# DeltaNet chunk inversion in four batches of five same-direction matrices, half of the columns, Y as the transpose of X

## The chip, the cores and the metric

The kernel runs on one core of a Trainium2 chip. The metric is the device time of one launch in microseconds (us). The kernel before was run three times.

## What is computed

One layer of a hybrid backbone: a gated DeltaNet in both directions over 1024 latent and 256 context tokens, windowed attention, a merge of the two, and a convolutional FFN. The change sits in the DeltaNet, which works head by head (8 heads of width 128). The part of the reference that matters is the triangular solve within a chunk:

```python
diff = gc[..., :, None] - gc[..., None, :]
decay = jnp.where(incl, jnp.exp(jnp.where(incl, diff, 0.0)), 0.0)
kk = jnp.einsum('nbhid,nbhjd->nbhij', kc, kc)
a_mat = jnp.where(strict, bc[..., :, None] * kk * decay, 0.0)
sol = lax.linalg.triangular_solve(a_mat, rhs, left_side=True, lower=True, unit_diagonal=True)
```

The kernel takes chunks of 128 tokens (10 of them) and, for each chunk and direction, inverts the unit triangular 128x128 matrix B itself, lower or upper by the direction. That is 20 inverses for each head.

## The kernel before

**Stages of a head.** `pe_prepare`, `dve_body`, `act_body` and `pool_body` hold the code of a head on the four engines. A head has four stretches: preparation (transposes, decays, the 20 matrices B in `b_full`, and a half precision copy `b_half`), the inversion (`pe_inverse`), one refinement of the inverse in full precision (the second half of `pe_inverse`), and the chain over the chunks (`pe_chain`), among whose steps the projections of the next head are laid (`pe_group`). A head's inversion waits for its preparation, and its chain for its refinement; nothing of another head lies beside the inversion on TensorE.

**The inversion.** X approaches the inverse of B by doubling the size of the diagonal blocks that are already inverted, in seven levels (block size 1, 2, ... 64); Y is kept as the transpose of X, since TensorE wants one operand transposed. A level makes P = B X, keeps the blocks of P that this level adds (a mask on VectorE, `p_masked`), and adds their product to X and Y. `BT` = 5 batches hold four 128x128 matrices each: two chunks, both directions. Level 0 needs only the mask (`x_half`), and Y of level 0 is a masked copy of B that GpSimd makes (`first_y`, L1743).

- TensorE, `p(n)` (L1274): 4 matmuls of 128 columns. `xy(n)`: X passed through an identity into PSUM (L1285, 512 columns), 4 matmuls of 128 columns on top (L1287), and the same for Y (L1289, L1291).
- VectorE, L1629: mask of 512 columns from PSUM to half precision, one for each batch and level.
- ScalarE, L1468 and L1469: X and Y back from PSUM, 512 columns each; in the last level as full precision, for the refinement.
- GpSimd, L1763: in the last level a half precision copy of Y.

Each engine runs its own list in order. `Count` objects are semaphores that only grow; `.wait` names the count to be reached. On TensorE `p` runs one batch ahead of `xy`, so that a mask has the time of one `xy` to be made:

```python
for n in range(BT + N + 1):
    if n < BT + N:
        p(n)
    if n >= BT + 1:
        xy(n - BT - 1)
```

**The refinement.** For each batch: residual product in full precision (L1306), its rounding on VectorE (L1637), a product with Y (L1317), the sum on VectorE (L1645).

**GpSimd.** `pool_body` copies the head's columns (L1723), makes two `g_masked` (L1732), puts ones on the diagonal of B as each batch comes (`affine_select`, L1749), the first Y, then splits the next head's weight tile for K (L177, L184). The tile for V is split only after the refinement, as `y_full` lies in its slot.

## Time and profile before

| | us |
|---|---|
| median of 3 runs | 3272.65 (3272.5 to 3274.65) |
| span of the profiled execution | 3268.6 |
| TensorE busy (matmul) | 2928.3, 90% |
| VectorE busy | 1503.2, 46% |
| ScalarE busy | 904.8, 28% |
| GpSimd busy | 700.1, 21% |

The span runs from the first to the last instruction of one profiled execution; the median of the timed runs is 4.05 us longer, which is what lies around the span. Matmuls are pipelined, and their records last longer than they hold the array, so the distance from start to start counts rather than their length. LDWEIGHTS, the load of the stationary operand, is a record of its own (PEld). PEclk is the granted clock as a share of 2.4 GHz.

### The profile page before, as it was taken

To read this page: it belongs to the slowest core of one execution; us is meant where nothing else is said; L and a number is where in the kernel's file an instruction comes from. 1 tells how busy PE (TensorE), PEld (TensorE's weight loads), DVE (VectorE), ACT (ScalarE), POOL (GpSimd) and SP (SyncE) were. 2 spreads that over 40 slices of the span, in tenths; PEclk is the share of its full clock that TensorE was granted. 3 is DMA by queue.
4 is the path that set the end of the run, shared out by engine and by line. 5 is a ranking of instruction groups with operands and counts; after the bars stand their busy time and mean duration, and the time that the engine had idled before them with its cause. 6 is when DMAs were issued, how large, how long until landed. Compare 5 with 4: busy or idle time off the path is not lost. (4 is left out here: it accounts for less than half of the span.)

```text
span 3268.6 us, 46436 instructions
## 1 busy us (share of the span) xinstructions
PE 2928.3 (90%) x17000; PEld 2430.4 (74%) x17000; DVE 1503.2 (46%) x2475; ACT 904.8 (28%) x1546; POOL 700.1 (21%) x545
## 2 busy tenths in 40 slices
PE   8599999799899899989899898869695999997999
PEld 7477788687678787878787777758574888886877
DVE  1474444300546565656565656631213555555242
ACT  1421333200251525252534343310113121222010
POOL 0241000132221213121212122023221232322221
PEclk7799899799889898999999899879897999998999
DMA  4110221221100001000000000032222111111433
GB/s 190 54 34 5 84 97 65 90 78 47 43 8 7 27 8 34 17 18 21 14 21 14 21 14 7 1 123 103 103 86 82 51 46 50 47 49 55 125 117 102
DMA packets 41784, 176.28 MB, mean 54 GB/s; under 512 B 4624, under 2 KB 4880, under 8 KB 39696
## 3 DMA queue, kind: packets, MB, share of 16 engines
q1 hardware_dynamic: 39312, 169.78, 15.4%
q10 hardware_dynamic: 2304, 4.20, 0.3%
q8 instruction: 114, 1.87, 0.2%
q14 instruction: 54, 0.44, 0.0%
HBM read 148.79 MB, written 25.17 MB: 53 GB/s over the span
## 5 line engine op out<-in xcount | busy, mean ns | idle before, releaser
L194 PE MATMUL ps_up<-h_hi,up_w_hi 128*128 128x512 f32 x704 | 274.6, 390 | 37.5 <-POOL up_w_lo L184 37.5
L195 PE MATMUL ps_up<-h_lo,up_w_hi 128*128 128x512 f32 x704 | 274.4, 390 | 0.0
L196 PE MATMUL ps_up<-h_hi,up_w_lo 128*128 128x512 f32 x704 | 274.4, 390 | 0.0
L1189 PE MATMUL dn_bank<-h_hi,dn_w_hi 128*128 128x512 f32 (+1 forms) x640 | 244.7, 382 | 12.8 <-POOL dn_w_lo L184 12.8
L1189 PE MATMUL dn_bank<-h_lo,dn_w_hi 128*128 128x512 f32 (+1 forms) x640 | 244.5, 382 | 0.0
L1189 PE MATMUL dn_bank<-h_hi,dn_w_lo 128*128 128x512 f32 (+1 forms) x640 | 244.4, 382 | 0.0
L1629 DVE TENSOR_TENSOR p_masked<-dn_bank,constants 128x512 f16<-128x512 f32 x240 | 165.9, 691 | 116.5 <-PE dn_bank L1274 115.5
L2017 DVE TENSOR_SCALAR ffn_u<-ffn_pad,vectors 128x1024 f32<-128x1024 f32 x44 | 103.9, 2360 | 232.2 <-ACT ffn_pad L1997 232.2
L194 PEld LDWEIGHTS ps_up<-h_hi,up_w_hi 128*128 128x128 f32 x704 | 132.6, 188 | 65.7 <-issue 38.3
L2086 PE MATMUL ps_down<-act_hi,down_w_hi 128*128 128x512 f32 x352 | 139.2, 395 | 24.4 <-DVE act_lo L2125 24.4
L195 PEld LDWEIGHTS ps_up<-h_lo,up_w_hi 128*128 128x128 f32 x704 | 132.6, 188 | 27.5
L196 PEld LDWEIGHTS ps_up<-h_hi,up_w_lo 128*128 128x128 f32 x704 | 132.5, 188 | 27.6
L1513 DVE SCALAR_TENSOR_TENSOR conv_out<-conv_in,head_taps,conv_out 128x1284 f32<-128x1284 f32 (+1 forms) x96 | 152.8, 1592 | 0.4
L1407 ACT ACTIVATE conv_in<-dn_bank 128x512 f32<-128x512 f32 (+1 forms) x64 | 34.9, 545 | 426.5 <-PE dn_bank L1189 420.2
L1189 PEld LDWEIGHTS dn_bank<-h_hi,dn_w_hi 128*128 128x128 f32 x640 | 122.1, 191 | 30.1 <-POOL dn_w_lo L184 13.2
L2087 PE MATMUL ps_down<-act_lo,down_w_hi 128*128 128x512 f32 x352 | 138.7, 394 | 0.0
L2088 PE MATMUL ps_down<-act_hi,down_w_lo 128*128 128x512 f32 x352 | 138.4, 393 | 0.0
L1468 ACT ACTIVATE x_half<-dn_bank 128x512 f16<-128x512 f32 x200 | 119.4, 597 | 59.9 <-PE dn_bank L1291 48.4
L1189 PEld LDWEIGHTS dn_bank<-h_hi,dn_w_lo 128*128 128x128 f32 x640 | 122.0, 191 | 17.0
L1189 PEld LDWEIGHTS dn_bank<-h_lo,dn_w_hi 128*128 128x128 f32 x640 | 122.1, 191 | 16.9
L184 DVE TENSOR_TENSOR down_w_lo<-down_w_raw,down_w_hi 128x1408 fp32r<-128x1408 f32 x32 | 52.0, 1626 | 161.2 <-POOL down_w_hi L177 161.2
L177 POOL CAST up_w_hi<-up_w_raw 128x1024 fp32r<-128x1024 f32 x44 | 45.7, 1039 | 371.4 <-PE ps_up L196 311.2
(317 smaller groups left out, 7122.1 us busy)
## 6 DMA issues: line engine op xcount, KB each, us to landing
up_w_raw<-in_w_up SPq DMA_DIRECT2D x44, 512.0 KB, 3.5
down_w_raw<-in_w_down SPq DMA_DIRECT2D x32, 704.0 KB, 4.2
late_w_ada<-in_w_ada SPq DMA_DIRECT2D x8, 2048.0 KB, 9.6
dn_w_raw<-in_w_dn SPq DMA_DIRECT2D x32, 512.0 KB, 3.8
w_ada<-in_w_ada SPq DMA_DIRECT2D x4, 2048.0 KB, 13.6
at_w_raw<-in_w_mg_at SPq DMA_DIRECT2D x16, 512.0 KB, 4.2
dnm_w_raw<-in_w_mg_dn SPq DMA_DIRECT2D x16, 512.0 KB, 5.2
x_in<-in_xT SPq DMA_DIRECT2D x8, 640.0 KB, 11.8
```

What stands on the lines that cost most here:

```text
L184: eng.tensor_tensor(self.lo[j][:, :, :], self.raw[j][:, :, :], self.hi[j][:, :, :].bitcast(F32), ALU.subtract).then_inc(self.split, 1)
L194: pe.matmul(out, self.hi[j][:, k, :], xh, start=(k == 0), stop=False)
L195: pe.matmul(out, self.hi[j][:, k, :], xl, start=False, stop=False)
L196: mm = pe.matmul(out, self.lo[j][:, k, :], xh, start=False, stop=(k == self.kt - 1))
L1189: mm = pe.matmul(bank[4 + s % 3][:, 0:n], wt[:, k, :], x[:, k, t0:t0 + n], start=(k == 0 and v == 0), stop=(k == KT - 1 and v == 2))
L1468: act.activation(flat(x_f if last else x_h, n % BT), bank[2 + n % 2][:, :], ACT.Copy)
L1513: ins = dve.scalar_tensor_tensor(out=dst, in0=src[:, j:j + n], scalar=taps[:, tile_at(tile), j:j + 1], in1=dst, op0=ALU.mult, op1=ALU.add)
L1629: dve.tensor_tensor(pm[:, (n - BT) % 2, :, :].rearrange("p (c d) n -> p c (d n)", c=2), p, mask, ALU.mult).then_inc(pmd.sem, 1)
L2017: ins = dve.tensor_scalar(u[:, s, :], src, tap(0), vec[:, bass.ds(m + s * FT + V_CONVB, 1)], ALU.mult, ALU.add)
L2086: pe.matmul(ps[j][:, :], w.hi[part][:, k, :], hi, start=(kk == 0), stop=False)
L2087: pe.matmul(ps[j][:, :], w.hi[part][:, k, :], lo, start=False, stop=False)
L2088: mm = pe.matmul(ps[j][:, :], w.lo[part][:, k, :], hi, start=False, stop=(kk == FT - 1))
```

## The change

A batch is now five matrices of one direction (`GC` = 5 chunks, `GB` = 4 batches). For a lower triangular X a level changes only columns in the even blocks, for an upper one only in the odd blocks; P, the mask, the product and the copy back take these 64 of 128 columns (`half`, `halves`, `packed`). Y is no longer updated by its own products: `y(n)` turns X by 5 matmuls with columns of an identity and copies the other half of the columns. X and Y start as identities that GpSimd writes (`units`). The copies of Y go by turns to ScalarE and VectorE. The last level leaves X in half precision; GpSimd widens the refinement's batches 0, 2 and 4 (`xfp`), ScalarE 1 and 3 (`xfa`), and the refinement adds to the half precision Y. GpSimd splits the next V tile before the end of the inversion. The constants lose nine 128x128 matrices.

```diff
         unit = 1.0 * (r == c) if level == 0 else 0.0
-        mats += [unit - m, unit - m.T]
-    mats += [mats[C_LEVEL + 1], mats[C_LEVEL]]
+        even = (np.arange(P) // s) % 2 == 0
+        mats.append(np.concatenate([(unit - m)[:, even], (unit - m.T)[:, ~even]], 1))
     mats = np.stack([np.broadcast_to(m, (P, P)) for m in mats], 1).astype(np.float32)
...
         size = NCH * 2 * P * 2
-        x_h, y_h = place("x_half", [P, NCH, 2, P], 0, F16), place("y_half", [P, NCH, 2, P], size, F16)
-        pm = place("p_masked", [P, 2, 4, P], 2 * size, F16)
-        e_h = place("residual_half", [P, 2, 4, P], 2 * size + 2048, F16)
-        b_h = place("b_half", [P, NCH, 2, P], cv_bytes, F16)
-        x_f = place("x_full", [P, NCH, 2, P], cv_bytes + size, F32)
-        y_full = [nc.alloc_sbuf_tensor_at(f"y_full{j}", [P, 2, 4 * P], F32, offset=ring + slot * tile_bytes)
-                  for j, slot in enumerate((Weights.HI + 1, Weights.LO + 1))]
-        y_f = [y_full[0][:, 0, :], y_full[0][:, 1, :], y_full[1][:, 0, :], y_full[1][:, 1, :],
-               o_norm[:, 0:4, :].rearrange("p m n -> p (m n)")]
-        assert 2 * size + 4096 <= cv_bytes and size * 3 <= pad_bytes + 2 * line
+        x_f = place("x_full", [P, NCH, 2, P], 0, F32)
+        pm = place("p_masked", [P, 2, GC, P // 2], 2 * size, F16)
+        e_h = place("residual_half", [P, 2, 4, P], 2 * size + 2560, F16)
+        x_h, y_h = place("x_half", [P, NCH, 2, P], cv_bytes, F16), place("y_half", [P, NCH, 2, P], cv_bytes + size, F16)
+        b_h = place("b_half", [P, NCH, 2, P], cv_bytes + 2 * size, F16)
+        assert 2 * size + 2560 + 2048 <= cv_bytes and size * 3 <= pad_bytes + 2 * line
         bank = [core.ps(f"dn_bank{b}", [P, HALF], ctx=st) for b in range(8)]
...
             return t[:, 2 * bt:2 * bt + 2, :, :]
+        def half(t, c, di, s, odd):
+            return t[:, c, di, :].rearrange("p (b two s) -> p b two s", two=2, s=s)[:, :, odd, :]
+        def halves(t, q, s, odd):
+            g, di = q // 2, q % 2
+            return t[:, g * GC:(g + 1) * GC, di, :].rearrange("p c (b two s) -> p c b two s", two=2, s=s)[:, :, :, odd, :]
+        def packed(b, s):
+            return bank[b][:, 0:GC * P // 2].rearrange("p (c b s) -> p c b s", c=GC, s=s)
...
+            def y_made(n):
+                if n % 2:
+                    ydv.wait(pe, h * YHALF + n // 2 + 1)
+                else:
+                    yac.wait(pe, h * YHALF + n // 2 + 1)
+            def x_made(n):
+                if n < GB:
+                    x1d.wait(pe, h * GB + n + 1)
+                else:
+                    xev.wait(pe, h * MSTEPS + n - GB + 1)
...
+                lv, q = divmod(n, GB)
+                g, di = q // 2, q % 2
...
+                    bhd.wait(pe, h * 5 + (5 if g else 3))
+                else:
+                    x_made(n - GB)
+                if 2 <= n < GB + 2:
+                    x1d.wait(pe, h * GB + n - 1)
+                elif n >= GB + 2:
+                    pmd.wait(pe, h * MSTEPS + n - GB - 1)
+                for i in range(GC):
+                    c = g * GC + i
+                    x = half(x_h, c, di, 1 << lv, di) if lv else core.id_h[:, di:P:2].unsqueeze(2)
+                    mm = pe.matmul(packed(n % 2, 1 << lv)[:, i], b_h[:, c, di, :], x, start=True, stop=True)
...
+            def x(n):
+                lv, q = divmod(n, GB)
+                g, di = q // 2, q % 2
+                pmd.wait(pe, h * MSTEPS + n - GB + 1)
+                y_made(n - GB)
+                if n >= GB + 2:
+                    xev.wait(pe, h * MSTEPS + n - GB - 1)
+                o = packed(2 + n % 2, 1 << lv)
+                pe.matmul(o, core.id_h[:, :], halves(x_h, q, 1 << lv, di), start=True, stop=False)
+                for i in range(GC):
+                    mm = pe.matmul(bank[2 + n % 2][:, i * P // 2:(i + 1) * P // 2], y_h[:, g * GC + i, di, :], pm[:, n % 2, i, :],
+                                   start=False, stop=(i == GC - 1))
+                mm.then_inc(xp.sem, 1)
+            def y(n):
+                lv, q = divmod(n, GB)
+                g, di = q // 2, q % 2
+                x_made(n)
+                if n >= 2:
+                    y_made(n - 2)
+                else:
+                    unit.wait(pe, h + 1)
+                turn = core.id_h[:, :].rearrange("p (b two s) -> p b two s", two=2, s=1 << lv)[:, :, 1 - di, :]
+                for i in range(GC):
+                    mm = pe.matmul(packed(6 + n % 2, 1 << lv)[:, i], x_h[:, g * GC + i, di, :], turn, start=True, stop=True)
+                mm.then_inc(yp.sem, 1)
+            for n in range(STEPS + 3):
+                if n < STEPS:
...
+                if GB < n <= STEPS:
+                    x(n - 1)
+                if n >= 3:
+                    y(n - 3)
...
+                    if bt % 2:
+                        xfa.wait(pe, h * 2 + bt // 2 + 1)
+                    else:
+                        xfp.wait(pe, h * 3 + bt // 2 + 1)
...
-                    yhd.wait(pe, h * 5 + b + 1)
+                    if b == 0:
+                        y_made(STEPS - 2)
+                        y_made(STEPS - 1)
...
-                    pmd.wait(pe, h * N + N)
+                    pmd.wait(pe, h * MSTEPS + MSTEPS)
...
                     act.activation(flat(b_h, bt - 1), flat(bf, bt - 1), ACT.Copy).then_inc(bhd.sem, 1)
-            for n in range(MERGES * BT):
-                last = n >= (MERGES - 1) * BT
-                xyp.wait(act, h * MERGES * BT + n + 1)
-                act.activation(flat(x_f if last else x_h, n % BT), bank[2 + n % 2][:, :], ACT.Copy)
-                act.activation(y_f[n % BT] if last else flat(y_h, n % BT), bank[6 + n % 2][:, :],
-                               ACT.Copy).then_inc(xyd.sem, 1)
+            for n in range(STEPS + 3):
+                if GB < n <= STEPS:
+                    lv, q = divmod(n - 1, GB)
+                    xp.wait(act, h * MSTEPS + n - GB)
+                    act.activation(halves(x_h, q, 1 << lv, q % 2), packed(2 + (n - 1) % 2, 1 << lv),
+                                   ACT.Copy).then_inc(xev.sem, 1)
+                if n >= 3 and n % 2:
+                    lv, q = divmod(n - 3, GB)
+                    yp.wait(act, h * STEPS + n - 2)
+                    act.activation(halves(y_h, q, 1 << lv, 1 - q % 2), packed(6, 1 << lv), ACT.Copy).then_inc(yac.sem, 1)
+            xev.wait(act, h * MSTEPS + MSTEPS)
+            for bt in (1, 3):
+                act.activation(flat(x_f, bt), flat(x_h, bt), ACT.Copy).then_inc(xfa.sem, 1)
             if fill:
...
+            for n in range(STEPS + 3):
+                if n < STEPS:
+                    lv, q = divmod(n, GB)
+                    mask = mats[:, C_LEVEL + lv, q % 2 * (P // 2):(q % 2 + 1) * (P // 2)].rearrange(
+                        "p (b s) -> p b s", s=1 << lv).unsqueeze(1).broadcast_to([P, GC, P // (2 << lv), 1 << lv])
+                    pd.wait(dve, h * STEPS + n + 1)
+                    if lv == 0:
+                        dve.tensor_tensor(halves(x_h, q, 1, q % 2), packed(n % 2, 1), mask, ALU.mult).then_inc(x1d.sem, 1)
+                    else:
+                        dve.tensor_tensor(pm[:, n % 2, :, :].rearrange("p c (b s) -> p c b s", s=1 << lv),
+                                          packed(n % 2, 1 << lv), mask, ALU.mult).then_inc(pmd.sem, 1)
+                if n >= 3 and n % 2 == 0:
+                    lv, q = divmod(n - 3, GB)
+                    yp.wait(dve, h * STEPS + n - 2)
+                    dve.tensor_copy(halves(y_h, q, 1 << lv, 1 - q % 2), packed(7, 1 << lv)).then_inc(ydv.sem, 1)
...
-            before = {T_K: -2, T_V: None, T_Q: TILE_END[T_K], T_GATE: TILE_END[T_V]}[tile]
-            by = (yfd, hn * 5) if tile == T_V else (grp, hn * NPROJ + before)
-            w.split_tile(pool, hn * 4 + tile, hn * 2 + tile // 2, tile % 2, by=by)
+            before = {T_K: -2, T_V: 0, T_Q: TILE_END[T_K], T_GATE: TILE_END[T_V]}[tile]
+            w.split_tile(pool, hn * 4 + tile, hn * 2 + tile // 2, tile % 2, by=(grp, hn * NPROJ + before))
...
-            def first_y(bt):
-                bfd.wait(pool, h * 5 + bt + 1)
-                kqc.wait(pool, h + 1)
+            def units():
+                cvs.wait(pool, h * 15 + 15)
+                bcd.wait(pool, h * 3 + 3)
+                ssd.wait(pool, h * 2 + 2)
...
-                mask = mats[:, C_FIRST_T:C_FIRST_T + 2, :].unsqueeze(1).broadcast_to([P, 2, 2, P])
-                pool.tensor_tensor(slots(y_h, bt), slots(bf, bt), mask, ALU.mult).then_inc(y1d.sem, 1)
+                one = core.id_h[:, :].unsqueeze(1).broadcast_to([P, 2 * NCH, P])
+                pool.tensor_copy(x_h[:, :, :, :].rearrange("p c d n -> p (c d) n"), one)
+                pool.tensor_copy(y_h[:, :, :, :].rearrange("p c d n -> p (c d) n"), one).then_inc(unit.sem, 1)
...
+            units()
...
-            for bt in range(BT):
-                first_y(bt)
...
-            for bt in range(BT):
-                xyd.wait(pool, (h + 1) * MERGES * BT - BT + bt + 1)
+                pool_split(pool, h + 1, T_V)
+            for bt in (0, 2, 4):
+                xev.wait(pool, h * MSTEPS + MSTEPS - (2 if bt == 0 else 0))
...
-                pool.tensor_copy(flat(y_h, bt), y_f[bt]).then_inc(yhd.sem, 1)
+                pool.tensor_copy(flat(x_f, bt), flat(x_h, bt)).then_inc(xfp.sem, 1)
...
-                pool_split(pool, h + 1, T_V)
...
-            for c in (colc, tapc, padz, bfd, gld, y1d, dgd, yhd, oz):
+            for c in (colc, tapc, padz, bfd, gld, dgd, xfp, unit, oz):
```

Where the order of work changes, engine by engine (`b_half` is B, `identity_half` a 128x128 identity, `dn_bank` PSUM). TensorE, one step of the loop in a middle level of the inversion, before:

```order
L1285 MATMUL dn_bank<-x_half,identity_half 128x512
L1287 MATMUL dn_bank<-p_masked,y_half 128x128 x4
L1289 MATMUL dn_bank<-y_half,identity_half 128x512
L1291 MATMUL dn_bank<-y_half,p_masked 128x128 x4
L1274 MATMUL dn_bank<-x_half,b_half 128x128 x4
L130 REGISTER_ALU
```

and now, two steps of the loop:

```order
L1315 MATMUL dn_bank<-x_half,identity_half 128x320
L1317 MATMUL dn_bank<-p_masked,y_half 128x64 x5
L1332 MATMUL dn_bank<-identity_half,x_half 128x64 x5
L1303 MATMUL dn_bank<-x_half,b_half 128x64 x5
L129 REGISTER_ALU x2
L1315 MATMUL dn_bank<-x_half,identity_half 128x320
L1317 MATMUL dn_bank<-p_masked,y_half 128x64 x5
```

Fourteen matmuls of a step, 2560 columns, have become sixteen with 1280, and the products that made Y have become the turns (L1332), which belong to a batch two steps back. VectorE in the same place, now (before, L1629 alone stood there, 512 columns each):

```order
L1680 TENSOR_TENSOR p_masked<-dn_bank,constants 128x320
L1685 CAST y_half<-dn_bank 128x5x64
L129 REGISTER_ALU
L1680 TENSOR_TENSOR p_masked<-dn_bank,constants 128x320
L129 REGISTER_ALU
```

Every second step a copy of Y stands between two masks. GpSimd at the start of a head, now:

```order
L1786 TENSOR_TENSOR g_masked<-constants,head_columns 128x512
L129 ISA x2
L129 REGISTER_ALU
L1798 COPY x_half<-identity_half 128x2560
L1799 COPY y_half<-identity_half 128x2560
L129 REGISTER_ALU
L1806 AFFINE_SELECT b_full<-b_full 128x512
```

The two copies of `units` stand between the second `g_masked` and the first `affine_select`; the five masked copies after the last `affine_select` are gone.

## Rows read from the trace of the kernel before

**Rows 1.** Busy by stretch, second head: stretch, length, PE, PEld, DVE, ACT, POOL, PEclk, DMA, GB/s.
```profile
1094.00:1134.40 40.40, 38.82 (x438) 28.59 (x439) 23.94 (x35) 31.76 (x59) 12.75 (x12) 0.92 0.05 15
1134.40:1142.60 8.20, 6.46 (x65) 5.89 (x63) 6.52 (x12) 1.42 (x3) 1.33 (x3) 1.00 0.00 0
```

**Rows 2.** Timeline, TensorE: first P, first X, first residual (start, length, idle before).
```profile
1093.99 0.61 PE L1274 MATMUL dn_bank<-identity_half,b_half 128*128 128x128 f16 x8 [1.72 <-issue]
...
1098.87 0.61 PE L1285 MATMUL dn_bank<-x_half,identity_half 128*128 128x512 f16 x1
...
1134.56 2.00 PE L1306 MATMUL dn_bank<-x_full,b_full 128*128 128x128 f32 x16
```

**Rows 3.** Timeline, TensorE: one step of a middle level.
```profile
1108.21 0.38 PE L1285 MATMUL dn_bank<-x_half,identity_half 128*128 128x512 f16 x1
1108.42 0.38 PE L1287 MATMUL dn_bank<-p_masked,y_half 128*128 128x128 f16 x4
...
1109.08 0.39 PE L1274 MATMUL dn_bank<-x_half,b_half 128*128 128x128 f16 x4
1109.31 0.38 PE L1285 MATMUL dn_bank<-x_half,identity_half 128*128 128x512 f16 x1
```

**Rows 4.** Timeline, ScalarE and VectorE in that step.
```profile
1108.08 0.60 ACT L1468 ACTIVATE x_half<-dn_bank 128x512 f16<-128x512 f32 x1
1108.58 0.59 ACT L1469 ACTIVATE y_half<-dn_bank 128x512 f16<-128x512 f32 x1
...
1109.60 0.69 DVE L1629 TENSOR_TENSOR p_masked<-dn_bank,constants 128x512 f16<-128x512 f32 x1 [0.51 <-PE dn_bank L1274]
```

**Rows 5.** Timeline and lines: 256 columns on VectorE and ScalarE, other stages.
```profile
1061.69 0.42 DVE L1549 TENSOR_TENSOR conv_out<-conv_out,dn_bank 128x256 f32<-128x256 f32 x1
1062.03 1.28 DVE L1513 SCALAR_TENSOR_TENSOR conv_out<-conv_in,head_taps,conv_out 128x1024 f32<-128x1024 f32 x1
...
L709 ACT ACTIVATE probs_t<-ps_probs_t 128x256 f32<-128x256 f32 x64 | 24.5, 383 | 47.6 <-PE ps_probs_t L647 47.6
```

**Rows 6.** Timeline, one narrow stretch: weight load, matmul, next weight load.
```profile
1116.42 0.10 PEld L1285 LDWEIGHTS dn_bank<-x_half,identity_half 128*128 128x128 f16 x1 [0.21 <-DVE p_masked L1629]
1116.44 0.10 PEld L1287 LDWEIGHTS dn_bank<-p_masked,y_half 128*128 128x128 f16 x1
1116.43 0.39 PE L1285 MATMUL dn_bank<-x_half,identity_half 128*128 128x512 f16 x1
```

**Rows 7.** Timeline, the last first-level masks and the matmuls they release.
```profile
1095.96 1.29 DVE L1625 TENSOR_TENSOR x_half<-dn_bank,constants 128x512 f16<-128x512 f32 x2 [0.26 <-PE dn_bank L1274]
1097.52 0.69 DVE L1625 TENSOR_TENSOR x_half<-dn_bank,constants 128x512 f16<-128x512 f32 x1 [0.26 <-PE dn_bank L1274]
...
1094.58 0.63 ACT L1464 ACTIVATE b_half<-b_full 128x512 f16<-128x512 f32 x1 [1.60 <-POOL b_full L1749]
...
1098.34 0.61 PE L1274 MATMUL dn_bank<-x_half,b_half 128*128 128x128 f16 x4 [0.35 <-DVE x_half L1625]
```

**Rows 8.** Busy by stretch: early in the inversion, and in the last head.
```profile
1097.00:1100.00 3.00, 2.65 (x18) 1.61 (x17) 2.24 (x4) 0.00 (x0) 3.00 (x4) 0.50 0.00 0
...
2082.00:2088.00 6.00, 4.30 (x45) 3.95 (x44) 5.84 (x11) 0.00 (x0) 0.00 (x0) 1.00 0.00 0
2088.00:2094.00 6.00, 5.71 (x20) 4.41 (x20) 3.62 (x12) 0.00 (x0) 0.00 (x0) 0.51 0.00 0
```

**Rows 9.** Timeline, GpSimd from the head's start on.
```profile
1069.59 2.04 POOL L1732 TENSOR_TENSOR g_masked<-constants,head_columns 128x512 f32<-128x512 f32 x2 [0.18 <-POOL head_columns L1723]
1081.64 0.63 POOL L1749 TENSOR_SCALAR_AFFINE_SELECT b_full<-b_full 128x512 f32<-128x512 f32 x1 [10.02 <-DVE b_full L1612]
...
1131.40 0.61 POOL L1763 CAST y_half<-y_full 128x512 f16<-128x512 f32 x1 [26.40 <-ACT y_full L1469]
```

**Rows 10.** DMA issue of the constants, and the stretch while it lands.
```profile
constants<-in_mats SPq DMA_DIRECT2D x1, 1600.0 KB, 7.2
...
5.00:10.00 5.00, 0.00 (x0) 0.00 (x0) 0.00 (x0) 0.22 (x1) 0.00 (x0) 1.00 0.99 412
```

More of the change, by code:

```diff
@@ L63 @@
 C_LEVEL = 9
-C_FIRST_T = C_LEVEL + 2 * LEVELS
-NCONST = C_FIRST_T + 2
+NCONST = C_LEVEL + LEVELS
 def constants():
@@ L1068 @@
 MERGES = LEVELS - 1
+GC = NCH // 2
+GB = 4
+STEPS = GB * LEVELS
+MSTEPS = GB * MERGES
+YHALF = STEPS // 2
 E_SCALE = 2048.0
@@ L1161, in delta_net @@
         colc, tapc, padz, bfd, oz = C("columns"), C("taps"), C("pad_zeroed"), C("b_with_i"), C("o_zeroed")
-        yhd = C("y_rounded")
-        gld, y1d, dgd = C("g_masked"), C("y_first"), C("k_rstd_diag")
+        xfp, unit = C("x_widened_pool"), C("x_and_y_units")
+        gld, dgd = C("g_masked"), C("k_rstd_diag")
         ystored, turns = core.sem("dn_y_stored"), core.sem("dn_pool_turns")
@@ L1267, in p @@
                 if lv == 0:
-                    bhd.wait(pe, h * 5 + bt + 1)
-                elif lv > 1:
-                    xyd.wait(pe, h * N + n - 2 * BT + 1)
-                for m in range(4):
-                    c, di = 2 * bt + m // 2, m % 2
-                    x = x_h[:, c, di, :] if lv else core.id_h[:, :]
-                    mm = pe.matmul(bank[n % 2][:, m * P:(m + 1) * P], b_h[:, c, di, :], x, start=True, stop=True)
-                mm.then_inc(pd.sem, 1)
-            def xy(n):
-                bt = n % BT
-                pmd.wait(pe, h * N + n + 1)
-                xyd.wait(pe, h * N + n - 1)
-                if n < BT:
-                    y1d.wait(pe, h * 5 + bt + 1)
-                bx, by = bank[2 + n % 2], bank[6 + n % 2]
-                pe.matmul(bx[:, :], core.id_h[:, :], flat(x_h, bt), start=True, stop=False)
-                for m in range(4):
-                    pe.matmul(bx[:, m * P:(m + 1) * P], y_h[:, 2 * bt + m // 2, m % 2, :], pm[:, n % 2, m, :],
-                              start=False, stop=(m == 3))
-                pe.matmul(by[:, :], core.id_h[:, :], flat(y_h, bt), start=True, stop=False)
-                for m in range(4):
-                    mm = pe.matmul(by[:, m * P:(m + 1) * P], pm[:, n % 2, m, :], y_h[:, 2 * bt + m // 2, m % 2, :],
-                                   start=False, stop=(m == 3))
-                mm.then_inc(xyp.sem, 1)
@@ L1301, in pe_inverse @@
                 if bt < BT:
-                    xyd.wait(pe, h * N + N - BT + bt + 1)
+                    if bt % 2:
+                        xfa.wait(pe, h * 2 + bt // 2 + 1)
+                    else:
+                        xfp.wait(pe, h * 3 + bt // 2 + 1)
                     ed.wait(pe, h * 5 + bt - 1)
@@ L1322, in pe_chain @@
             yfd.wait(pe, h * 5 + 5)
-            xyd.wait(pe, h * MERGES * BT + MERGES * BT)
+            xev.wait(pe, h * MSTEPS + MSTEPS)
             kqc.wait(pe, h + 1)
@@ L1371, in tensor @@
         def tensor(pe):
-            for c in (grp, ssd, bcd, tr, dps, kqd, pd, xyp, rd_, y2d, ksd, xrd, oqd, otd):
+            for c in (grp, ssd, bcd, tr, dps, kqd, pd, xp, yp, rd_, y2d, ksd, xrd, oqd, otd):
                 c.open(pe)
@@ L1486, in scalar @@
         def scalar(act):
-            for c in (evac, sil, sqd, stdc, tka, kqc, dct, bhd, xyd, osq):
+            for c in (evac, sil, sqd, stdc, tka, kqc, dct, bhd, xev, yac, xfa, osq):
                 c.open(act)
@@ L1644, in dve_body @@
                     y2d.wait(dve, h * 5 + b + 1)
-                    dve.scalar_tensor_tensor(out=flat(bf, b), in0=bank[b % 2][:, :], scalar=1.0 / E_SCALE, in1=y_f[b],
+                    dve.scalar_tensor_tensor(out=flat(bf, b), in0=bank[b % 2][:, :], scalar=1.0 / E_SCALE, in1=flat(y_h, b),
                                              op0=ALU.mult, op1=ALU.add).then_inc(yfd.sem, 1)
@@ L1677, in vector @@
         def vector(dve):
-            for c in (qsd, ovr, cvs, rec, nrm, tkd, bqd, x1d, pmd, ed, yfd, rdy, vd, stt, o1, od, orec, onr, fin):
+            for c in (qsd, ovr, cvs, rec, nrm, tkd, bqd, x1d, pmd, ydv, ed, yfd, rdy, vd, stt, o1, od, orec, onr, fin):
                 c.open(dve)
```

27 lines of the change are left out of this document (3 added, 24 removed).

## The prediction

> **What bounds the kernel now.** I read the busy times first, then the stretches of one head, then the timeline of each engine within one step of the inversion, and last the few rows that price narrower work.
>
> The inversion stretch of the second head lasts 40.4 us with TensorE busy 38.8 and ScalarE 31.8 of them, and the refinement behind it 8.2 us [rows 1]. Nothing of another head lies beside it, so a microsecond less in that stretch is one less in the kernel, eight times. The marks I reckon with are the first P at 1093.99, the first X at 1098.87 and the first residual product at 1134.56 [rows 2]. From first P to first residual that is 40.57 us, and I take this head for all eight.
>
> Between the first X and the first residual lie 30 steps, so 1.19 us each. In a step of a middle level TensorE goes from one X to the next in 1.10 us: 0.21 for the 512 columns through the identity, 0.22 for each group of four 128-column matmuls, five such blocks back to back [rows 3]. ScalarE starts two copies 0.50 us apart, of 0.60 us each [rows 4]. So TensorE bounds it, with ScalarE close behind, and VectorE's mask of 0.69 us has slack.
>
> **What a narrow matmul costs.** Everything hangs on this. Four loads with 128 columns behind each take 0.22 us, 54 ns a pair [rows 3]; that is 128 columns at the full clock, so it says nothing of 64. Two weight loads in half precision stand 0.02 us apart, with the matmul between them starting 0.01 us after the first [rows 6]: the load itself seems to take little of the array. So a pair with 64 columns costs between 27 ns (half of 54, columns alone) and 54 ns (the width hidden behind load and issue). I take 40 ns, the middle: at 27 ns TensorE would have to be fed 32 instructions a step, one in 14 ns, longer than the two or three that one sees in a burst.
>
> A page says otherwise in both directions. The Trainium skill, "TensorE: Matmul & The Clock Gate", section "Back-to-back issue gap", gives about 81 ns for a load and matmul at 128 columns in a sustained stream, and in its table about 25 ns for anything up to 64. By 81 ns the new step would be slower than the old one; the trace disagrees with its 54 ns. By 25 ns an estimate of the new step is near my lower bound.
>
> **The new step.** TensorE: P is 5 pairs, 0.20 us; X is 320 columns (0.21 x 320/512 = 0.13) and 5 pairs, 0.33; the turn is 5 pairs, 0.20. Together 0.73 us.
>
> VectorE: 256 columns take 0.42 us with the next start 0.34 later [rows 5], 512 take 0.69 with 0.60 between starts [rows 7]. For 320 that gives 0.49 long and 0.40 held. Two masks and a copy of Y in two steps: 1.2 us, 0.60 a step. ScalarE: 0.38 us for 256 [rows 5] and 0.60 for 512 [rows 4] give 0.44 for 320, 0.34 held, three in two steps, 0.51 a step. Both below TensorE.
>
> But the batches are only four, and a mask now comes back later than TensorE needs it. The loop is: X of a batch starts; 0.33 later the turn, 0.20 later P of the batch after next, whose last matmul starts after 0.16 and takes about 0.19 (0.22 less 27 ns): 0.88. To VectorE 0.13 [rows 3, 4], mask 0.49, back to TensorE 0.13 [rows 7], where a prefetched load makes it 0.05 [rows 6]; I take 0.10. That is 1.60 us for two steps, **0.80 us a step**. VectorE's copy of Y falls between two masks and fits, as 1.2 is below 1.6.
>
> **The length of the inversion.** The first P waits for the preparation as before and starts at 1094.0 [rows 2]. The second group of chunks waits for the fifth copy of B, 1094.58 + 0.63 = 1095.2 [rows 7], so P of batches 2 and 3 follows by 1095.9, their masks end about 1096.9, P of level 1 ends about 1096.95, its mask 1097.55, and the first X starts at 1097.65, 1.2 us earlier than now. Then 23 steps lead to the last X. TensorE's clock stands at 0.50 from 1097 to 1100 [rows 8], and I let it stay there until 1101.65. A step at half clock is 1.08 us (columns cost double: 0.27, 0.54, 0.27), so 4.0 us hold 3.7 steps; the other 19.3 take 15.4. The last X starts at 1117.1. Its copy on ScalarE (0.33 + 0.19 + 0.05 + 0.44 + 0.10) and the last turn put the first residual 1.3 us behind it: 1118.4. Against 1134.56 that is **16.2 us a head, 129 us in eight**.
>
> **What else it touches.**
> - Units on GpSimd: two copies of 2560 columns. GpSimd casts 512 in 0.61 us [rows 9], so about 1.2 ns a column and 3 us each, 6 us. They start after the second `g_masked`, at 1071.6, and GpSimd is idle for 10.0 us until 1081.64 [rows 9]. They cost nothing; with half that speed they would delay the first `affine_select` by 2 us, and P with it.
> - The five masked copies for Y go, and the V tile is split in their place. At nothing: after them GpSimd waited 26.4 us for the last level [rows 9], and that slack covers the split; without it the widening would come late.
> - Widening of X: 0.63 us on ScalarE as for B [rows 7], 0.61 on GpSimd [rows 9]. Batch 0 waits only until the second group's X is left, and is ready in time; batch 1 is ready about 2.1 us after the last X starts, when the first residual (1.3 + 0.94) is through. At nothing; at most 0.6 us a head, 5 us, if one of them is late.
> - The refinement itself keeps its operations, 8.2 us.
> - Constants: 9 of 25 matrices less, 576 KB of 1600 KB. At the 412 GB/s of that stretch 1.4 us, at 1600 KB in 7.2 us 2.6 us [rows 10]. The first use of x waits behind them. I take 1.4 us.
>
> The sum: 129 + 1.4 = 131 us less. The profiled span of 3268.6 becomes 3137.6; the 4.05 us around it, the distance to the median of the three runs, stay: 3272.65 - 131 = **3142 us**.
>
> **Bounds.** With pairs at 27 ns the loop gives 0.71 us a step and 3128 us; if the clock rises at once as well, 3117. If VectorE alone were the bound (0.60 a step, no half clock) 3098. With pairs at 54 ns TensorE needs 0.94 us a step, at half clock 1.87, and the first residual comes at 1122.6: 97 us less with the constants, 3175.
>
> **The rivals.**
> - A, issue or load bound: a narrow pair costs what a wide one does. For it: no narrow half precision matmul in the trace; every second step has one register instruction more, and its wait holds TensorE's queue. Against it: the loads 0.02 us apart. 3175 us. Worse still (A2) if a stream of loads costs half as much again, 80 ns a pair: a step of 15 x 0.08 + 0.13 = 1.33 us, first residual at 1129.5, 3231 us. Against that stand the 54 ns [rows 3]. A2 is what the section of the Trainium skill named above would give.
> - B, the clock: TensorE now pauses in each step, where it was busy 96% of the stretch. In the last head a stretch with it busy 4.3 of 6 us at full clock was followed by one at 0.51 [rows 8]. If half of the inversion runs at half clock, the step is (0.80 + 1.08)/2 = 0.94 us, 113 us less, and the chain begins at half clock, perhaps 2 us a head given back: 3175 us. Against it: in the refinement busy 6.46 of 8.20 us kept the clock at 1.00 [rows 1].
> - C, fine pieces: in levels 0 to 2 the copies write runs of 1, 2 and 4 half precision columns. If they take twice as long there, ScalarE holds 3 x 0.68 / 2 = 1.02 us a step and bounds 12 steps, 12 x 0.22 = 2.6 us a head: 3163. No row has such a pattern, for or against.
> - D, the other side: both A and B in full. Pairs that cost a whole load at half clock, a clock that never rises because of the waits: 1.87 us a step, 23 steps, first residual at 1142, 7.4 us later a head, 59 us slower: 3330. The point from which the change loses is a step of (1134.56 - 1097.65 - 1.3)/23 = 1.55 us.
> - E, it does not do what it says: if waits between copies of Y and X make the four batches run one after the other, each level costs a full loop: P 0.35, to VectorE 0.13, mask 0.49, back 0.10, X 0.50, copy 0.59, turn 0.35, copy 0.59, 3.1 us, and the other three batches half a step each behind it, some 4.7 us in four steps. At 1.2 us a step the first residual comes at 1126.6: 3207. The waits allow two steps ahead, so I give it little.
>
> **Chances.** Forecast with a step of 0.70 to 0.85 us: 51%. Faster than that: 8%. A 14%, A2 2%, B 13%, C 6%, E 3%, D 3%. Range 3110 to 3185: it takes in the low bounds short of VectorE alone, A, B and C, and leaves out A2, D, E and combinations of A with B. About 0.2% (6.5 us) is what a measurement tells from no change; all cases but D lie beyond it on the faster side: faster 0.96, same 0.01, slower 0.03.
>
> **What would show it.** Right: the stretch from first P to first residual at 24 to 25 us in each head; X through the identity coming every 0.80 us on average; narrow matmuls 40 ns apart; VectorE busy about three quarters of it; the refinement at 8.2 us; GpSimd's unit copies over before the first `affine_select`. Wrong: narrow matmuls at 54 ns or more (A); a granted clock below 0.9 in the inversion or below 1 in the refinement (B); masks of the first levels longer than 0.49 us, or turns slower than those of the last levels (C); the first `affine_select` late; residual products waiting for `x_full`.

## The result and the profile after

| | before | changed |
|---|---|---|
| median | 3272.57 us (3268.08 to 3274.65, 4 runs) | 3143.97 us (3137.65 to 3154.32, 4 runs) |
| ratio | | 0.9619, 95% interval 0.9596 to 0.9642 |
| span of the profiled execution, mean clock | 3268.6 us, 0.917 | 3135.8 us, 0.916 |

The kernel is 3.8% faster, 128.6 us by the medians; 131 us were forecast. The profiled execution is the fastest of its four runs (3137.65, so 1.85 us lie around the span, not the 4.05 that I kept), and its span is 132.8 us shorter. The page of the changed kernel, its part 1:

```profile
PE 2777.6 (89%) x16872; PEld 2333.4 (74%) x16872; DVE 1459.5 (47%) x2531; ACT 775.3 (25%) x1386; POOL 676.8 (22%) x505
```

TensorE lost 150.7 us of busy time, more than the kernel did: it now stands idle inside the inversion, where it was busy 38.8 of 40.4 us [rows 1]. The second head, timeline of TensorE: first P, first X, the X that follow, last X, first residual.

```profile
1071.63 0.46 PE L1303 MATMUL dn_bank<-identity_half,b_half 128*128 128x64 f16 x10 [1.52 <-issue]
...
1075.10 0.45 PE L1315 MATMUL dn_bank<-x_half,identity_half 128*128 128x320 f16 x1 [0.26 <-DVE p_masked L1680]
...
1076.16 0.46 PE L1315 MATMUL dn_bank<-x_half,identity_half 128*128 128x320 f16 x1
...
1077.22 0.46 PE L1315 MATMUL dn_bank<-x_half,identity_half 128*128 128x320 f16 x1
...
1094.13 0.31 PE L1315 MATMUL dn_bank<-x_half,identity_half 128*128 128x320 f16 x1 [0.41 <-DVE p_masked L1680]
...
1095.63 2.02 PE L1351 MATMUL dn_bank<-x_full,b_full 128*128 128x128 f32 x16
```

From first P to first residual that is 24.00 us against 40.57 [rows 2]. In all eight heads it lies between 23.7 and 24.7 us (before 39.8 to 41.1). Added up over the heads, profile against profile:

| part | before | after | difference |
|---|---|---|---|
| start to first head's first P | 937.5 | 930.9 | -6.6 |
| first P to first residual, eight heads | 322.3 | 192.3 | -129.9 |
| first residual to the chain's first product | 65.0 | 66.2 | +1.2 |
| chain | 510.1 | 514.5 | +4.4 |
| rest (preparations between, and the end) | | | -1.8 |

(Differences are taken before rounding.)

The chains take one of two lengths in both kernels, 66.3 to 66.4 or 67.9 to 68.0 us, the last head's being shorter; two of the first seven were long before, four now. The longer ones hold a piece at a lower clock: over the second head's chain of 67.96 us the granted clock is 0.97 in the mean, over the first head's of 66.38 us it is 1.00. Busy by stretch, changed kernel, in two stretches of the inversion, in the refinement, and in such a chain (columns as in [rows 1]):

```profile
1075.00:1078.00 3.00, 2.90 (x43) 2.54 (x44) 2.07 (x5) 1.32 (x4) 2.92 (x3) 0.50 0.06 15
...
1081.00:1096.00 15.00, 12.56 (x291) 10.59 (x287) 11.63 (x27) 11.74 (x30) 1.39 (x3) 1.00 0.11 38
...
1096.00:1104.00 8.00, 6.05 (x60) 5.50 (x60) 6.78 (x13) 0.42 (x1) 0.46 (x3) 1.00 0.01 2
1164.00:1168.00 4.00, 4.00 (x15) 3.34 (x14) 2.92 (x7) 1.18 (x1) 2.33 (x1) 0.63 0.00 0
```

**The inversion's step.** One round of the loop is two steps ("the turn" below is always the five matmuls of L1332, which turn X into Y). TensorE, then VectorE and ScalarE, changed kernel, second head:

```profile
1084.62 0.31 PE L1315 MATMUL dn_bank<-x_half,identity_half 128*128 128x320 f16 x1 [0.15 <-DVE p_masked L1680]
1084.76 0.31 PE L1317 MATMUL dn_bank<-p_masked,y_half 128*128 128x64 f16 x5
1084.91 0.31 PE L1332 MATMUL dn_bank<-identity_half,x_half 128*128 128x64 f16 x5
1085.06 0.31 PE L1303 MATMUL dn_bank<-x_half,b_half 128*128 128x64 f16 x5
1085.28 0.30 PE L1315 MATMUL dn_bank<-x_half,identity_half 128*128 128x320 f16 x1
...
1086.20 0.31 PE L1315 MATMUL dn_bank<-x_half,identity_half 128*128 128x320 f16 x1 [0.19 <-DVE p_masked L1680]
```

```profile
1085.26 0.49 DVE L1685 CAST y_half<-dn_bank 128x320 f16<-128x320 f32 x1 [0.26 <-PE dn_bank L1332]
1085.66 0.88 DVE L1680 TENSOR_TENSOR p_masked<-dn_bank,constants 128x320 f16<-128x320 f32 x2
```

```profile
1085.76 0.44 ACT L1516 ACTIVATE x_half<-dn_bank 128x320 f16<-128x320 f32 x1 [0.22 <-PE dn_bank L1317]
1086.10 0.43 ACT L1521 ACTIVATE y_half<-dn_bank 128x320 f16<-128x320 f32 x1
```

Blocks of five narrow matmuls start 0.145 us apart, 29 ns a pair, and TensorE's work in a step, the 320 columns of X and three blocks of five, is 4 x 0.145 = 0.58 us. Two steps take 1086.20 - 1084.62 = 1.58 us, 0.79 a step. The path goes: X starts at 1084.62; the turn of an older batch is over at 1084.91 + 0.31 = 1085.22; VectorE's copy of that turn starts at 1085.26; the mask behind it in VectorE's queue starts at 1085.66 and is over at 1086.15; the next but one X starts at 1086.20. The P that this mask reads was over at 1085.06 + 0.31 = 1085.37; with the same 0.04 for the handing over, the mask started 0.25 us later than P allowed, because VectorE was at the copy. That is not the loop of the prediction, in which the mask starts when P is done.

All X products together (the view of one line's instructions, changed kernel):

```profile
L1315 PE MATMUL dn_bank<-x_half,identity_half x192: 296/309/455, 934.3 to 1944.7; 128*128 128x320 f16 x192
its engine sat idle before it (us, times) until:
  DVE p_masked L1680: 42.1, 139
```

42 us of idle time in 184 steps, 0.23 each, end with VectorE's mask: 0.58 + 0.23 is 0.81. The mean hides a pattern: with the clock at full, an X whose mask stands behind a copy mostly starts 0.85 to 1.00 us after the X before it, and one whose mask does not 0.58 to 0.73.

### The profile page after: what moved, and what is told of

Same layout as the page of the kernel before. It is cut to its first block and busy times, and to the rows that moved or that the text cites. A ratio compares the mean times of both kernels' runs of the same rounds, so it can differ in the third digit from the quotient of the medians.

```text
span 3135.8 us, 45853 instructions
## 1 busy us (share of the span) xinstructions
PE 2777.6 (89%) x16872; PEld 2333.4 (74%) x16872; DVE 1459.5 (47%) x2531; ACT 775.3 (25%) x1386; POOL 676.8 (22%) x505
## 5 line engine op out<-in xcount | busy, mean ns | idle before, releaser
L2076 DVE SCALAR_TENSOR_TENSOR ffn_u<-ffn_pad,vectors,ffn_u 128x1024 f32<-128x1024 f32 x88 | 113.0, 1285 | 12.8 <-DVE ffn_u L2076 0.2
L2052 ACT ACTIVATE ffn_pad<-ps_up 128x1024 f32<-128x1024 f32 x44 | 45.3, 1029 | 285.0 <-PE ps_up L195 284.9
```

The lines of the kernel that those rows point to most:

```text
L2076: ins = dve.scalar_tensor_tensor(out=u[:, s, :], in0=src, scalar=tap(n), in1=u[:, s, :], op0=ALU.mult, op1=ALU.add)
```

## The experiments

Two theories of what sets the step of 0.79 us. **T**: X waits for VectorE, which must do the copy of a turn and then the mask, and the turn stands behind X on TensorE. **P**: the loop of the prediction, through P and its mask, with the copy beside it. A third, **E**: TensorE's own instruction stream. (As names of theories P and E are neither the product P nor the rival E of the prediction.) "Step" is the distance from first to last X over 23, as the mean of the eight heads, with the half clock at the head's start in it; P to R is the sum over eight heads of first P to first residual. The changed kernel has 0.828 us and 192.3 us.

| run | median us | ratio (95%) | step | P to R |
|---|---|---|---|---|
| changed again | 3144.77 | 0.9622 (0.9598 to 0.9646) | 0.833 | 193.8 |
| turns on ScalarE | 3135.43 | 0.9565 (0.9528 to 0.9601) | 0.794 | 186.3 |
| more matmuls behind P | 3147.77 | 0.9604 (0.9569 to 0.9638) | 0.832 | 194.1 |
| more matmuls before P | 3149.75 | 0.9605 (0.9568 to 0.9642) | 0.864 | 200.0 |
| more matmuls before the turn | 3155.59 | 0.9632 (0.9594 to 0.9669) | 0.916 | 209.7 |
| VectorE's copy behind the mask | 3158.98 | 0.9642 (0.9629 to 0.9655) | 0.920 | 209.5 |
| turn before X | 3128.92 | 0.9574 (0.9550 to 0.9598) | 0.773 | 181.1 |
| the same, ScalarE too | 3124.99 | 0.9562 (0.9539 to 0.9585) | 0.690 | 164.5 |
| constants back | 3148.29 | 0.9632 (0.9610 to 0.9655) | 0.833 | 193.7 |

The median moves by several us with the lengths of the chains, so the step and P to R of the profiles carry the verdicts. Both contain the steps at half clock, whose number differs from head to head, and in two runs (more matmuls behind P, and before P) also single stalls of TensorE, one of 0.74 us with no releaser in the profile. The last twelve steps of a head are at full clock; their mean, as the median of the eight heads, is 0.79 us in the changed kernel, both times, and with the constants back, 0.75 with the turns on ScalarE, 0.79, 0.83 and 0.865 with more matmuls behind P, before P and before the turn, 0.88 with the copy behind the mask, 0.74 and 0.66 with the turn before X.

**1. All copies of Y on ScalarE.** VectorE keeps only the masks.

```diff
-                if n >= 3 and n % 2:
+                if n >= 3:
...
-                    act.activation(halves(y_h, q, 1 << lv, 1 - q % 2), packed(6, 1 << lv), ACT.Copy).then_inc(yac.sem, 1)
+                    act.activation(halves(y_h, q, 1 << lv, 1 - q % 2), packed(6 + (n - 3) % 2, 1 << lv), ACT.Copy).then_inc(yac.sem, 1)
```

> The changed kernel, with every copy of Y on ScalarE and none on VectorE. In the profile of the changed kernel a step takes 0.79 us in the second head, TensorE's work in it 0.58. Theory T (the loop runs X, turn, VectorE's copy of the turn, mask, X): without the copy the mask waits for P alone, x start + 0.75 + 0.05 + 0.49 + 0.05 = 1.34 us in two steps; ScalarE holds 2 x 0.34 = 0.68 a step. A step of 0.68 to 0.72, 2 us less a head, about 15 us less in all. Theory P of the forecast (the loop runs X, P, mask, X, and VectorE's copy fits beside it): the step stays at 0.79, no change, or slower, as ScalarE has more to do. Theory E (TensorE's work sets the step): no change.

The step fell by 0.035 us, less than T gave and against P. The wait went to another engine. Idle time of TensorE before X, and ScalarE in the last head, this run:

```profile
  ACT y_half L1518: 16.1, 59
  DVE p_masked L1677: 6.6, 31
```

```profile
1928.97 0.43 ACT L1518 ACTIVATE y_half<-dn_bank 128x320 f16<-128x320 f32 x1
1929.29 0.44 ACT L1513 ACTIVATE x_half<-dn_bank 128x320 f16<-128x320 f32 x1
1929.62 0.44 ACT L1518 ACTIVATE y_half<-dn_bank 128x320 f16<-128x320 f32 x1
```

The mask's 42.1 us have become 6.6; ScalarE now has two copies a step, held 0.32 to 0.33 us each and nearly without a gap, and most of the waits that the profile names end with its copy of Y. In that last head two steps take 1.34 us, T's number (ScalarE's four copies alone would hold it to much the same, 1.3); in the middle heads they take 1.50. More on these under 2.

**2. Five more matmuls a step, at three places.** They write an unused PSUM bank, and nothing is left out. Behind P, before P, or between X and the turn:

```diff
+            def extra(n):
...
+                for i in range(GC):
+                    pe.matmul(bank[4][:, i * P // 2:(i + 1) * P // 2], b_h[:, g * GC + i, di, :], core.id_h[:, 0:P // 2], start=True, stop=True)
```

> The changed kernel with five more matmuls of 64 columns in every step behind P (24 a head), into a PSUM bank that nobody reads; 0.145 us of TensorE a step. Theory T and theory P: the work falls into the time in which TensorE waits for the mask; no change, at most 3 us. Theory E: 24 x 8 x 0.145 = 28 us slower.

> The same five matmuls, but ahead of P in each step, so that P ends 0.145 us later behind X. Theory P: the loop X, P, mask, X grows by 0.145 in two steps, 0.07 x 24 x 8 = 14 us slower. Theory T: P has 0.24 us of slack before the mask it is read by, so no change, at most 3 us. Theory E: 28 us slower.

> The same five matmuls between X and the turn of each step, so that both the turn and P come 0.145 us later. Theory T: the loop X, turn, copy, mask, X grows by 0.145 in two steps, 14 us slower. Theory P: 14 us slower as well. Theory E: 28 us slower. With the run that has them ahead of P it tells T from P.

The same work costs 0.00, 0.04 and 0.09 us a step as the table has it, and 0.00, 0.03 and 0.07 at full clock. Idle time of TensorE before X, with the matmuls behind P:

```profile
  DVE p_masked L1688: 5.2, 16
```

Behind P they fill the wait for the mask (42.1 us of it shrink to 5.2) and the step stays: E falls, for the steps at full clock. (At half clock such a step grew from 1.06 to 1.33 us; there TensorE is the bound.) Before the turn they delay the copy, and with it mask and X, by their whole length, 0.145 us in two steps or 0.07 a step; both theories have that, since the turn stands ahead of P, so this run doesn't part them.

Before P, T gave nothing and P 0.07; in the first seven heads 0.03 was measured at full clock, between the two, and in the last head nothing: 0.79 us a step, T's number. The timeline of a middle head tells what happened there. TensorE, then VectorE, that run:

```profile
1086.47 0.30 PE L1315 MATMUL dn_bank<-x_half,identity_half 128*128 128x320 f16 x1
...
1087.04 0.31 PE L1303 MATMUL dn_bank<-x_half,b_half 128*128 128x64 f16 x5
...
1088.12 0.30 PE L1315 MATMUL dn_bank<-x_half,identity_half 128*128 128x320 f16 x1
```

```profile
1087.39 0.49 DVE L1688 TENSOR_TENSOR p_masked<-dn_bank,constants 128x320 f16<-128x320 f32 x1 [0.32 <-PE dn_bank L1303]
1087.82 0.49 DVE L1693 CAST y_half<-dn_bank 128x320 f16<-128x320 f32 x1
```

The loop has fallen into another pattern: here the mask starts as soon as P is over (1087.35), with the copy behind it, and X starts 0.24 us behind the mask's end at 1087.88, where the X shown of the changed kernel has 0.06 (0.05 by its rounded times). So two loops lie close together. The one through the copy takes 1.58 us for two steps; the one through P takes 1.33 (1.58 less P's wait of 0.25), and with the extra block and those 0.19 more 1.33 + 0.145 + 0.19 = 1.66, which is the 1.65 seen. The release of 0.24 us appears with the turns on ScalarE too, and is why that run, whose loop goes through P alone, stayed above T's number in the middle heads: 0.74 + 0.03 + 0.49 + 0.24 = 1.50 for two steps, 0.75 each. That run, a mask and the X behind it, second head and last head:

```profile
1089.07 1.08 DVE L1677 TENSOR_TENSOR p_masked<-dn_bank,constants 128x320 f16<-128x320 f32 x2 [0.43 <-PE dn_bank L1300]
1089.80 0.30 PE L1312 MATMUL dn_bank<-x_half,identity_half 128*128 128x320 f16 x1 [0.18 <-DVE p_masked L1677]
...
1929.59 0.49 DVE L1677 TENSOR_TENSOR p_masked<-dn_bank,constants 128x320 f16<-128x320 f32 x1 [0.17 <-PE dn_bank L1300]
1930.16 0.30 PE L1312 MATMUL dn_bank<-x_half,identity_half 128*128 128x320 f16 x1
```

The first mask of the pair is over at 1089.56 and its X starts 0.24 us later; the one at 1929.59 is over at 1930.08, and X starts after 0.08. From the sixth X of each head on, the median is 0.24 us for the 133 of the first seven heads and 0.08 for the 19 of the last. The trace also has TensorE's queue instructions, which the views above leave out. The first seven heads are one loop in the program, and before each of those 133 X a register instruction (L129) takes over the wait for the mask: it starts 0.04 us behind the mask's end, at 1089.60, a semaphore instruction follows at 1089.70, X's weight load at 1089.77, X at 1089.80. The last head stands outside that loop and has no register instruction there. In the changed kernel the 70 X of the first seven heads whose mask stands behind a copy start 0.06 us behind it, and there no register instruction stands between. So the 0.24 us go with a register instruction between mask and X. No run changes that alone.

**3. VectorE's copy behind the mask.** This one parts them most clearly. The copy of each odd turn is put behind the next mask, not ahead of it:

```diff
-                if n >= 3 and n % 2 == 0:
-                    lv, q = divmod(n - 3, GB)
-                    yp.wait(dve, h * STEPS + n - 2)
+                if n >= 5 and n % 2:
+                    lv, q = divmod(n - 4, GB)
+                    yp.wait(dve, h * STEPS + n - 3)
```

> VectorE copies Y behind the next mask instead of ahead of it; nothing else changes. In the changed kernel (second head, one turn of two steps) TensorE has P ready 0.25 us before its mask starts, because VectorE holds the copy of Y first. T: the next X needs both the mask and that copy, so the loop is P, mask held 0.40, copy 0.49, X: from an X 0.75 to the end of P, 0.04, 0.40, 0.49, 0.05 = 1.73 us for two steps instead of 1.58, so a step of about 0.86 to 0.90 instead of 0.83 us as the mean of the heads (half clock at the head's start included), the median 5 to 15 us longer; X now waits for VectorE's y_half where it waited for p_masked. P (the path is P and its mask, and the copy only stands in its way by the order of VectorE's queue): 1.33 us for two steps, a step of about 0.71, and the median 15 to 25 us shorter.

Two steps now take 1.77 us in the second head, 0.04 above what T gave. The mean step of 0.920 lies a little above T's 0.86 to 0.90, at full clock it is 0.88, and P's 0.71 is far off. The median is 14 us longer than that of the changed kernel (another chip; by the ratios, whose intervals just overlap, some 6 us). TensorE and VectorE, this run:

```profile
1089.23 0.30 PE L1315 MATMUL dn_bank<-x_half,identity_half 128*128 128x320 f16 x1 [0.42 <-issue]
...
1091.00 0.30 PE L1315 MATMUL dn_bank<-x_half,identity_half 128*128 128x320 f16 x1 [0.40 <-issue]
```

```profile
1090.01 0.49 DVE L1680 TENSOR_TENSOR p_masked<-dn_bank,constants 128x320 f16<-128x320 f32 x1 [0.48 <-PE dn_bank L1303]
1090.42 0.48 DVE L1685 CAST y_half<-dn_bank 128x320 f16<-128x320 f32 x1
1090.82 0.48 DVE L1680 TENSOR_TENSOR p_masked<-dn_bank,constants 128x320 f16<-128x320 f32 x1
```

The mask ends at 1090.50, and X doesn't start: it starts at 1091.00, 0.10 behind the copy's end (1090.90). The view names no releaser, but in the trace a semaphore instruction of TensorE's queue waits from 1090.23 to 1090.95 for ScalarE's copies of X and for this copy of Y, and goes on 0.05 us behind the copy's end. P and its mask alone are not the path of the changed kernel, or X would have come earlier; mask and copy both stand before the same X, in either order. (That X needs both stands in the program: `x` waits for `y_made`. What the run adds is that the time goes there.)

**4. The turn before X on TensorE.** If the copy of the turn belongs to the loop, an earlier turn shortens it. X's own wait for its bank is then covered by the turn's and goes too:

```diff
-                if n >= GB + 2:
-                    xev.wait(pe, h * MSTEPS + n - GB - 1)
...
-                if GB < n <= STEPS:
-                    x(n - 1)
                 if n >= 3:
                     y(n - 3)
+                if GB < n <= STEPS:
+                    x(n - 1)
```

In the second kernel ScalarE also copies Y ahead of X (its two blocks change places).

> The changed kernel with the turn ahead of X in each step of TensorE's loop; X's wait for its own bank falls away, as the turn has waited for the same copy. Theory T: the copy of the turn no longer hangs behind X, and P follows X at once. Loop: X 0.29, last matmul of P 0.12 + 0.19, 0.05, mask 0.49, 0.05 = 1.19 us in two steps; VectorE holds 0.60 a step, TensorE 0.58. A step of 0.60 to 0.66 us, 23 x 0.15 = 3.5 us less a head, some 28 us less in all: 3112 to 3120 us. Theory P of the forecast: P comes earlier too, 0.145 less in two steps, a step of 0.72, 14 us less.

> As the run before it, and ScalarE too copies the turn ahead of X. ScalarE holds 0.51 us a step either way. If the copy of X is what the next turn waits for (0.99 us behind X, against about 1.03 in the order), this one is slower than the other by up to 0.05 us a step, 10 us; if the copy of the turn is late, faster. I expect no difference of over 3 us.

The first gave 0.773 us, far less than T promised. The mask's wait was gone, but a new one stood before the turn. Idle time of TensorE before the turn, first kernel, and ScalarE there:

```profile
  ACT y_half L1519: 25.4, 93
```

```profile
1090.22 0.44 ACT L1514 ACTIVATE x_half<-dn_bank 128x320 f16<-128x320 f32 x1 [0.41 <-PE dn_bank L1315]
1090.55 0.43 ACT L1519 ACTIVATE y_half<-dn_bank 128x320 f16<-128x320 f32 x1
```

ScalarE held the copy of Y behind a copy of X that waited for its product, and the next turn into that bank waited for the copy of Y. With ScalarE's order changed to match TensorE's, which I had expected to matter by no more than 3 us, this wait went too. TensorE in the second kernel:

```profile
1088.29 0.31 PE L1313 MATMUL dn_bank<-x_half,identity_half 128*128 128x320 f16 x1
...
1088.93 0.30 PE L1313 MATMUL dn_bank<-x_half,identity_half 128*128 128x320 f16 x1
...
1089.55 0.31 PE L1313 MATMUL dn_bank<-x_half,identity_half 128*128 128x320 f16 x1
...
1090.22 0.30 PE L1313 MATMUL dn_bank<-x_half,identity_half 128*128 128x320 f16 x1
```

Steps of 0.64 us, with 0.58 of work in them. P to R is 28 us shorter than in the changed kernel (29 against its second profile), and the median 19.8 us below the same kernel's runs on the same chip (3119.02 to 3130.18 against 3142.11 to 3151.54). It computes what the changed kernel does and beats both.

**5. Constants, and the changed kernel again.** Nine unused matrices are put back into the table:

```diff
-NCONST = C_LEVEL + LEVELS
+NCONST = C_LEVEL + LEVELS + 9
...
+    mats += [1.0 * (r == c)] * 9
```

> The changed kernel with nine unused 128x128 matrices added to the constants, so that they are 1600 KB again. In the profile of the changed kernel the constants were in 1.96 us earlier and the first inversion started 6.6 us earlier. If the smaller constants make all of that: 6.6 us slower, first P at 937.5. If only the landing counts, and the rest is the clock's phase, which differs from run to run: 2 us slower, too little to tell from the timed runs, but silu_c back at 8.4 us in the profile.

> The changed kernel as it is, for its spread and as the base of this group. Its four runs so far lie between 3137.65 and 3154.32 us; expected median 3138 to 3152, the inversion 24 us a head, the start of the first head's inversion between 931 and 938 us, the chain 66.4 or 68.0 us from head to head.

The constants landed 2.1 us later than without them. First use (ScalarE's timeline), the changed kernel again, and with the matrices back:

```profile
6.16 0.22 ACT L276 ACTIVATE silu_c<-vectors 128x16 f32<-128x16 f32 x1 [4.12 <-DMA constants<-in_mats]
```

```profile
8.24 0.22 ACT L277 ACTIVATE silu_c<-vectors 128x16 f32<-128x16 f32 x1 [6.21 <-DMA constants<-in_mats]
```

Yet the first head's first P came at 935.3 us with them and at 936.8 without, where the first profile of the changed kernel had 930.9. The medians differ by 3.5 us with intervals that overlap. So the 2 us at the start are real, and of the 6.6 us by which the first head came earlier the rest varies from one execution to the next.

## Why the prediction was right

3143.97 us was measured and 3142.0 forecast, and the mechanism (less work in each step, a loop over four batches as the bound instead of TensorE's work) holds, but the path through that loop was wrong, and the step's number came out by luck: two errors cancel. No run takes the change apart, so how much the half columns, the turn in place of Y's own products and the four batches each gave is not shown. The steps of the prediction one by one:

- **The step, 0.80 us a step by the loop X, turn, P, mask.** Measured 0.79, but this is two errors that cancel. A narrow pair costs 29 ns, not 40, so TensorE's share of a step is 0.58 and not 0.73 us. And "VectorE's copy of Y falls between two masks and fits" failed: VectorE had the time, as 1.2 us in 1.6 says, but not at the place. The copy waits for the turn and holds up a mask whose P is done, and the next X needs both. By this trace the loop that I wrote takes 1.33 us, 0.67 a step; the right one with my sizes 0.33 + 0.16 + 0.19 to the turn's end, 0.13, copy held 0.40, mask 0.49, 0.10: 1.80, 0.90 a step. Experiments 3 and 4 show the copy in the loop, and so does the last head with more matmuls before P, where those cost nothing.
- **A narrow pair, 40 ns between 27 and 54.** 29 ns in every block, near the lower bound. That TensorE would then be fed one instruction in 14 ns was no obstacle. The Trainium skill's "TensorE: Matmul & The Clock Gate", section "Back-to-back issue gap", gives 25 ns as a floor up to 64 columns, and the 29 ns are near it; its 81 ns for a load and matmul in a stream is not seen here, at 128 columns (54 ns [rows 3]) or at 64.
- **VectorE 0.49 and 0.40, ScalarE 0.44 and 0.34.** Measured 0.49 and 0.40, 0.44 and 0.33.
- **First X 3.65 us behind first P.** Measured 3.47.
- **Half clock until 4.0 us behind the first X, a step of 1.08 there.** Steps were 1.06 us; the clock rose about 3.1 us behind the first X. 23 steps took 19.03 us against 19.4.
- **Last X to first residual 1.3 us.** Measured 1.50: the last turn waited 0.53 us for a copy of Y on VectorE.
- **16.2 us a head, 129 in eight.** Measured 129.9.
- **Units on GpSimd, 6 us hidden in the idle 10.** They take 2.32 us each, and the idle time ahead of the first `affine_select` is still 5.39 us. Changed kernel, GpSimd:

```profile
1048.88 2.32 POOL L1798 COPY x_half<-identity_half 128x2560 f16<-128x2560 f16 x1
1051.13 2.32 POOL L1799 COPY y_half<-identity_half 128x2560 f16<-128x2560 f16 x1
1058.85 0.64 POOL L1806 TENSOR_SCALAR_AFFINE_SELECT b_full<-b_full 128x512 f32<-128x512 f32 x1 [5.39 <-DVE b_full L1666]
```

- **Widening of X at nothing, refinement 8.2 us.** The first residual started behind the last turn, and the refinements took 8.0 to 8.4 us.
- **Constants 1.4 us.** About 2.0, by experiment 5; still below the upper bound of 2.6.
- **The chain, at no change.** 4.4 us longer in the profile, by which chains fall into a lower clock. In the second profile of the changed kernel four of the first seven were long again, partly others, and the chains add up to 511.8 us. What makes a chain long was not tested.

The rivals. A and A2 fall with the 29 ns. B, the clock: in the inversion's later part and in the refinement the granted clock is 1.00, with TensorE busy 12.56 of 15 and 6.05 of 8 us. C, fine pieces: ScalarE's 192 copies of X write pieces of 2 to 64 columns and last 437 to 445 ns throughout. Single columns, in the first level, do cost something: 526 to 537 ns for ScalarE's 16 copies of Y there against 432 to 434 for its 96 others, 506 to 530 against 490 to 494 on VectorE, and 504 to 524 for the masks, against 467 to 493 for those that write their 320 columns in one piece (L1680). That is far from the doubling in three levels that the rival asked for. Lines of VectorE and ScalarE, changed kernel:

```profile
L1680 DVE TENSOR_TENSOR p_masked<-dn_bank,constants x192: 467/481/493, 933.7 to 1944.1; 128x320 f16<-128x320 f32 x192
```

```profile
L1678 DVE TENSOR_TENSOR x_half<-dn_bank,constants x32: 504/514/524, 931.2 to 1924.5; 128x320 f16<-128x320 f32 x32
```

```profile
L1516 ACT ACTIVATE x_half<-dn_bank x192: 437/437/445, 934.8 to 1945.2; 128x320 f16<-128x320 f32 x192
```

E, batches in series: X comes every 0.79 us, not 1.2. D needed A and B.

## What to carry to other kernels

In a ring of engines, follow for one turn every instruction that the next step needs, in the order of each queue: whether an engine has time left over says nothing of whether the work stands at the right place. When two engines share a ring, give them the same order; here, changing TensorE's alone moved the wait to ScalarE, and changing ScalarE's with it gave the rest. A total that comes out right does not prove its terms: here the width of a matmul and the path of the loop were both wrong, in opposite directions.

## What the runs showed of the hardware

- A half precision load with a matmul of 64 columns takes 29 ns in a block of five, against 54 ns at 128 columns [rows 3]: at full clock the time goes with the columns down to 64.
- At half clock (0.50, 1.2 GHz) blocks of five take 0.27 us instead of 0.145 and a step 1.06 instead of 0.79, though its waits for VectorE and ScalarE do not grow: TensorE is then the bound.
- Written pieces of two columns or more cost VectorE and ScalarE next to nothing: 0.47 to 0.49 us for a mask that writes 320 columns in one piece, 0.44 on ScalarE for every copy of X, in pieces of 2 to 64. In single columns a mask takes 0.50 to 0.52 and a copy on ScalarE 0.53 instead of 0.43.
- X starts 0.06 us behind its mask in the changed kernel where nothing of TensorE's queue stands between, 0.08 in the last head with the turns on ScalarE, and 0.24 where a register instruction of the loop takes over the wait for the mask (133 of that run's X, one median). Both cases occur within one run; no run isolates it.
